# A two-block transformer on one core: x loaded in four pieces between the first weight halves, the positions loaded as rows and turned by small products, and the first quarters ordered by channel half

## The reference

```python
def rms_norm(x, g):
    y = xf * lax.rsqrt(jnp.mean(xf * xf, axis=-1, keepdims=True) + NORM_EPS)
    return (y * g.astype(jnp.float32)).astype(x.dtype)

def rope_tables(positions):
    inv_freq = ROPE_THETA ** (-jnp.arange(0, ROT_DIM, 2, dtype=jnp.float32) / ROT_DIM)
    ang = positions.astype(jnp.float32)[..., None] * inv_freq
    return jnp.cos(ang)[:, None], jnp.sin(ang)[:, None]

def moba_attention(xn, w_qkv, w_o, cos, sin):
    qkv = (xn @ w_qkv).reshape(b, s, 3, N_HEADS, HEAD_DIM)
    ...
xn = rms_norm(x, norm_mix[i])
y = moba_attention(xn, attn_w_qkv[i_attn], attn_w_o[i_attn], cos, sin)
```

## Time and profile before

| | before |
|---|---|
| median of 3 runs (lowest to highest) | 1083.42 us (1083.03 to 1083.55) |
| the profiled execution's own time | 1084.0 us |
| its span, first to last instruction | 1082.1 us |
| TensorE matmuls busy in the span | 1068.2 us (99%) |
| VectorE, ScalarE busy | 740.3 us (68%), 561.6 us (52%) |
| moved by DMA | 195.84 MB, mean 181 GB/s |

### The profile page before, as it was taken

The page is one execution under the profiler, slowest core; times in us unless marked ns, Lnnn a source line. Parts: engine busy times, 40 slices in busy tenths (PEclk is TensorE's granted clock), DMA queues, the critical chain, the costliest instruction groups (busy, mean ns, idle before and its releaser), DMA issues.

```text
span 1082.1 us, 15291 instructions
## 1 busy us (share of the span) xinstructions
PE 1068.2 (99%) x5810; PEld 908.3 (84%) x5810; DVE 740.3 (68%) x1044; ACT 561.6 (52%) x725; POOL 40.7 (4%) x61
## 2 busy tenths in 40 slices
PE   8999999999999999999999999999999999999997
PEld 6888888888888888889888888888889778888886
DVE  5756674655786656558897966666897879566665
ACT  5556443434455435346675554445654766444453
POOL 1000000000000000000000220000300200000000
PEclk9999999999999999999999999999999999999999
DMA  9953266465447465646533665657576324654651
GB/s 333 336 174 112 86 216 217 166 203 184 159 140 257 158 215 171 202 137 184 194 120 102 213 206 177 195 187 239 152 254 225 81 79 163 226 193 157 207 179 39
DMA packets 127163, 195.84 MB, mean 181 GB/s; under 512 B 6977, under 2 KB 97217, under 8 KB 126994
## 3 DMA queue, kind: packets, MB, share of 16 engines
q1 hardware_dynamic: 123904, 185.77, 51.6%
q0 software_dynamic: 3216, 9.51, 2.9%
q10 hardware_dynamic: 2, 0.00, 0.0%
HBM read 194.21 MB, written 1.05 MB: 180 GB/s over the span
## 4 chain that ended last, share of the span: by engine, by line
PE 94%; DVE 4%; ACT 1%; issue 1%; DVEq 0%; DMA 0%; ACTq 0%
PE ps L2108 26%; PE ps L2009 15%; PE ps L2011 15%; PE ps L2010 15%; PE ps L2111 13%; PE ps L2190 2%; PE ps L2229 1%; PE ps L2051 1%; PE ps L2192 1%; PE ps L2255 1%; PE ps L2641 1%; DVE act L1246 1%; PE ps L2288 1%; DVE wlo L1121 1%; PE ps L2469 0%
## 5 line engine op out<-in xcount | busy, mean ns | idle before, releaser
L2108 PE MATMUL ps<-act,whi 128*128 128x512 f32 x1200 | 424.7, 397 | 0.0
L1121 DVE TENSOR_TENSOR wlo<-raw,whi 128x2048 fp32r<-128x2048 f32 (+2 forms) x161 | 364.0, 2277 | 87.2 <-ACT whi L678 86.8
L2111 PE MATMUL ps<-act,wlo 128*128 128x256 f32 x1200 | 336.6, 281 | 0.0
L678 ACT ACTIVATE whi<-raw 128x2048 fp32r<-128x2048 f32 (+2 forms) x170 | 317.5, 1887 | 26.2 <-PE ps L2011 21.2
L2108 PEld LDWEIGHTS ps<-act,whi 128*128 128x128 f32 x1200 | 225.3, 188 | 54.0
L2111 PEld LDWEIGHTS ps<-act,wlo 128*128 128x128 f32 x1200 | 226.7, 189 | 2.0
L2011 PE MATMUL ps<-whi,hlo 128*128 128x512 f32 x400 | 157.3, 393 | 0.0
L2010 PE MATMUL ps<-wlo,hhi 128*128 128x512 f32 x400 | 156.7, 392 | 0.0
L2009 PE MATMUL ps<-whi,hhi 128*128 128x512 f32 x400 | 156.4, 391 | 0.1
L2009 PE MATMUL ps<-whi,act 128*128 128x512 f32 (+2 forms) x286 | 112.4, 393 | 1.5 <-DVE act L1821 0.6
L2011 PE MATMUL ps<-whi,act 128*128 128x512 f32 (+2 forms) x286 | 108.0, 378 | 0.0
(11 more groups left out here) (232 smaller groups left out, 1153.8 us busy)
## 6 DMA issues: line engine op xcount, KB each, us to landing
raw<-mlp_w_up_in SPq DMA_DIRECT2D x32, 1024.0 KB, 6.3
raw<-mlp_w_down_in SPq DMA_DIRECT2D x32, 1024.0 KB, 4.9
raw<-ffn_w_gate_in SPq DMA_DIRECT2D x22, 1024.0 KB, 5.3
raw<-ffn_w_up_in SPq DMA_DIRECT2D x22, 1024.0 KB, 5.4
raw<-ffn_w_down_in SPq DMA_DIRECT2D x22, 1024.0 KB, 4.8
raw<-attn_w_qkv_in SPq DMA_DIRECT2D x10, 1024.0 KB, 8.9
raw<-w_kv_shared_in SPq DMA_DIRECT2D x8, 1024.0 KB, 5.3
raw<-attn_w_o_in SPq DMA_DIRECT2D x4, 1024.0 KB, 4.9
```

The lines of the kernel that those rows point to most:

```text
L678: nc.scalar.activation(whi[:, s, 0:width], raw[:, s, 0:width], ACT.Copy).then_inc(hi_ready, 1)
L1121: nc.vector.tensor_tensor(wlo[:, s, 0:width], raw[:, s, 0:width], whi[:, s, 0:width].bitcast(F32), ALU.subtract).then_inc(lo_ready, 1)
L2108: nc.tensor.matmul(bank(b + f), lhsT=w[0][:, at:at + P], rhs=act[:, k, :, :].rearrange("p a t -> p (a t)"), start=k == 0, stop=False, skip ...
L2111: ins = nc.tensor.matmul(bank(b + f, 0, T), lhsT=w[1][:, at:at + P], rhs=act_hi[:, k, :], start=False, stop=k == KT - 1, skip_group_check= ...
```

## The change

SP loads x in four pieces of 256 KB, each one quarter, between the weight halves. The quarters of the first norm are now ordered by channel half: quarters 0 and 1 are the token tiles 0 and 1 of channels 0 to 511, quarters 2 and 3 those of the other channels. ACT's queue loads the two position arrays as rows of 256 integers on one partition, behind the gain row; POOL's two loads go. VectorE converts the 512 integers at the head of its list; TensorE turns them into columns by four products with a 1x1 one, and VectorE copies the four columns. The second half of the gain row is spread after the first quarter's transposes. Five identity products stand ahead of the first quarter, none later. `qkv_products` of chunk 0 takes one token tile after the other, with the transposes of quarters 1, 2 and 3 in between.

```diff
+        pos_row_i = arena[0:1, 0:512].bitcast(I32)
+        pos_row = arena[0:1, 512:1024]
...
-        BY_TILES = ("mix0", "mlp0", "mix1", "mlp1", "fpre0", "kvsrc", "fpre1")
+        BY_TILES = ("mlp0", "mix1", "mlp1", "fpre0", "kvsrc", "fpre1")
...
-            sp.dma_start(x[:, 0, :], x_rows[:, 0, :]).then_inc(x_loaded, 16)
+            def load_x(p):
+                h, t, cols = quarter("mix0", p)
+                sp.dma_start(x[:, t, cols], x_rows[:, t, cols]).then_inc(x_loaded[p], 16)
+
+            load_x(0)
             load_half(0, 0, first_half_loaded)
-            sp.dma_start(x[:, 1, :], x_rows[:, 1, :]).then_inc(x_rest_loaded, 16)
             load_half(0, 1, w_loaded[SLOT[0]])
+            load_x(1)
             load_half(1, 0, second_half_loaded)
+            load_x(2)
             load_half(1, 1, w_loaded[SLOT[1]])
+            load_x(3)
...
-            for n, name in enumerate(("positions", "positions_2")):
-                pool.dma_start(pos_i[:, n, :], a[name].rearrange("a (t p) -> p (a t)", p=P),
-                               allow_slow_non_contiguous=True).then_inc(pos_loaded, 16)
...
+            for n, name in enumerate(("positions", "positions_2")):
+                act.dma_start(pos_row_i[:, n * T:(n + 1) * T], a[name]).then_inc(pos_loaded, 16)
...
+            hi_part_of(0, 0, first_half_loaded, first_half_hi)
             copy_turned("mix0", (0,))
-            hi_part_of(0, 0, first_half_loaded, first_half_hi)
-            copy_turned("mix0", (1, 2))
             hi_part_of(0, 1, w_loaded[SLOT[0]], hi_ready)
             hi_part_of(1, 0, second_half_loaded, second_half_hi)
-            copy_turned("mix0", (3,))
+            copy_turned("mix0", (1,))
             hi_part_of(1, 1, w_loaded[SLOT[1]], hi_ready)
+            copy_turned("mix0", (2, 3))
...
+            dve.wait_ge(pos_loaded, 32)
+            nc.vector.tensor_copy(pos_row, pos_row_i).then_inc(pos_row_made, 1)
             dve.wait_ge(first_row_spread, 1)
...
+            nc.vector.tensor_copy(pos_f[:, :, :].rearrange("p n t -> p (n t)"), bank(7, 0, 2 * TT)).then_inc(pos_copied, 1)
...
-            dve.wait_ge(pos_loaded, 32)
-            link(nc.vector.tensor_copy(pos_f[:, :, :], pos_i[:, :, :]))
+            dve.wait_ge(pos_copied, 1)
...
+            spread_first_row(0)
+            pe.wait_ge(const_loaded, 16)
+            warm(5)
+            turn("mix0", parts=(0,))
+            spread_first_row(1)
+            pe.wait_ge(pos_row_made, 1)
+            for n in range(2 * TT):
+                ins = nc.tensor.matmul(bank(7, n, n + 1), lhsT=pos_row[:, n * P:(n + 1) * P], rhs=scale_row[0:1, 0:1],
+                                       start=True, stop=True)
...
-                    for h in range(2):
-                        pe.wait_ge(*((lo_ready, c + 1) if h else (half_lo, 1)))
-                        for t in range(TT):
-                            if h == 0:
-                                wait_acts("mix0", c + 1 + 2 * t)
+                    for t in range(TT):
+                        wait_acts("mix0", 2 * c + t + 1)
+                        for h in range(2):
+                            pe.wait_ge(*((lo_ready, c + 1) if h else (half_lo, 1)))
...
-                            if c == 0 and h == 0 and t == 1:
-                                turn("mix0", parts=(3,))
+                            if c == 0 and t <= h:
+                                turn("mix0", parts=(1 + h + t,))
```

More of the change, by code:

```diff
@@ L236, in two_blocks @@
         row_used = sem("row_used")
-        x_loaded = sem("x_loaded")
-        x_rest_loaded = sem("x_rest_loaded")
+        x_loaded = [sem(f"x_loaded{p}") for p in range(4)]
         second_half_loaded = sem("second_half_loaded")
@@ L246, in two_blocks @@
         pos_loaded = sem("pos_loaded")
+        pos_row_made = sem("pos_row_made")
+        pos_turned = sem("pos_turned")
+        pos_copied = sem("pos_copied")
         bias_loaded = [sem(f"bias_loaded{s}") for s in range(8)]
@@ L1616, in lo_part_of @@
                                         whi[:, SLOT[c], cols].bitcast(F32), ALU.subtract).then_inc(done, 1)
+            dve.wait_ge(pos_loaded, 32)
+            nc.vector.tensor_copy(pos_row, pos_row_i).then_inc(pos_row_made, 1)
             dve.wait_ge(first_row_spread, 1)
-            dve.wait_ge(x_loaded, 16)
-            dve.sem_inc(x_ready, 2)
+            dve.wait_ge(x_loaded[0], 16)
             first_gained(0)
+            lo_part_of(0, 0, first_half_hi, 1, first_half_lo)
+            split_turned("mix0", (0,))
+            dve.wait_ge(x_loaded[1], 16)
             first_gained(1)
-            split_turned("mix0", (0,))
-            dve.wait_ge(x_rest_loaded, 16)
+            lo_part_of(0, 1, hi_ready, 1, lo_ready)
+            dve.wait_ge(first_row_spread, 2)
+            dve.wait_ge(pos_turned, 1)
+            nc.vector.tensor_copy(pos_f[:, :, :].rearrange("p n t -> p (n t)"), bank(7, 0, 2 * TT)).then_inc(pos_copied, 1)
+            dve.wait_ge(x_loaded[2], 16)
             dve.sem_inc(x_ready, 2)
             first_gained(2)
-            lo_part_of(0, 0, first_half_hi, 1, first_half_lo)
             split_turned("mix0", (1,))
+            lo_part_of(1, 0, second_half_hi, 1, second_half_lo)
+            split_turned("mix0", (2,))
+            dve.wait_ge(x_loaded[3], 16)
+            dve.sem_inc(x_ready, 2)
             first_gained(3)
-            split_turned("mix0", (2,))
-            lo_part_of(0, 1, hi_ready, 1, lo_ready)
+            lo_part_of(1, 1, hi_ready, 2, lo_ready)
             dve.wait_ge(xs_ready, 4 * XSR["mix0"] + 4)
             release_row()
-            lo_part_of(1, 0, second_half_hi, 1, second_half_lo)
             split_turned("mix0", (3,))
-            lo_part_of(1, 1, hi_ready, 2, lo_ready)
             cursor[0] = 2
@@ L2031, in turn @@
             def turn(name, blocks=((0, 4), (4, 8)), parts=range(4)):
-                if name == "mix0" and 0 in parts:
-                    pe.wait_ge(ones_made, 1)
-                    pe.wait_ge(first_row_loaded, 16)
-                    for h in range(2):
[L2037 to L2040, removed]
                 for p in parts:
                     h, t, _ = quarter(name, p)
-                    if name == "mix0":
-                        for _ in range((3, 0, 3, 0)[p]):
-                            nc.tensor.matmul(bank(7, 0, P), lhsT=ident, rhs=ident, start=True, stop=True)
                     if name in BUSY:
@@ L2399, in ffn_layer, with spread_first_row, warm @@
                 last_downs(f, n0 + 31, n0 + 32, NF, then, (5, 6) if then else ())
-            turn("mix0", parts=(0, 1, 2))
+            def spread_first_row(h):
+                nc.tensor.matmul(bank(2 + h), lhsT=scale_row[0:1, 0:P], rhs=rows[0:1, 0, h * HALF:(h + 1) * HALF],
+                                 start=True, stop=True).then_inc(first_row_spread, 1)
+            def warm(n):
+                for _ in range(n):
+                    nc.tensor.matmul(bank(7, 0, P), lhsT=ident, rhs=ident, start=True, stop=True)
+            pe.wait_ge(ones_made, 1)
+            pe.wait_ge(first_row_loaded, 16)
+            spread_first_row(0)
[7 more added lines that the diff above has]
+                                       start=True, stop=True)
+            ins.then_inc(pos_turned, 1)
             def qkv_products(i, kh):
```

1 line of the change is left out of this document (removed).

## The result

The change makes the kernel slower: 1088.23 us (median of 6 runs, 1085.65 to 1088.56) against 1083.49 us of the kernel before (6 runs, 1083.03 to 1084.45). The forecast was 1083.7, with a range to 1085.9. The profiled execution took 1088.55 us with a span of 1086.1, against 1084.0 and 1082.1.

The account below looks back on a forecast made before the run. TensorE was taken to bound the kernel. Chunk 2's high part 0.79 later, less 0.17 for the conversion and 0.30 of cover, starts chunk 4 0.32 later: 1083.42 + 0.32 = 1083.7 us, range 1082.0 to 1085.9.

Parts of the forecast that it names:

- the other road: VectorE's path to the first product, through the first quarter's copy and low part: ready at 9.0, shorter than TensorE's.
- the rival of late positions: Positions land after 5.2 and hold VectorE's whole queue; at worst first product 2.5 later, 1086.2 us; chance 0.06.
- The new wait: TensorE idle ahead of chunk 4 until VectorE's copy of the first result: about 0.32 + 0.8 = 1.1 us.
- the second tile of x: Landed at 9.2; its late landing held the third quarter's gain product, hence the low part ahead of the first product.
- the 5.74 for 24 products: TensorE's time for 24 products and one more turn after the last quarter's turn at 16.71, ending about 22.8.
- TensorE goes faster at about 9.1: TensorE's step from lower to upper level comes at about 9.1, as in the earlier trace, after the second half-row's passes start.
- the position passes: Eight TensorE passes ahead of the first product, priced at the upper level: 0.90 us, first product at 10.14.
- from the first product to the last turn: TensorE's four groups of six products and turns in chunk 0: 6.57 us, last quarter turned at 16.71.
- the chain behind: From ScalarE's high part of chunk 2 to VectorE's copy ahead of chunk 4: 17.15 us without slack, less 0.17 for the conversion.
- the slow level: TensorE stays at its lower level through the one-row products: 1084.5 with no slow product, 1085.8 with six; chance 0.14.

Follow-up runs that it names:

- the control: The kernel before with chunk 4's high and low parts put ahead of the sine and cosine: 1083.79 us, ratio 1.0001.
- The pair of fillings: Changed kernel with both half-rows first, positions behind the last quarter, plus six products in TensorE's gap: identity 1086.08 us, one-row 1088.61 us.

## Why the prediction was wrong

**What held.** The first transposes start at 6.58, as forecast. The first quarter's low part ends at 8.31 + 0.69 = 9.00, as the other road had it. The conversion ended at 4.01, before the 5.2 at which it would cost (0.41 us, between its bounds), so the rival of late positions fell. From the last turn to chunk 2's high part it took 1.13 (forecast 1.12), and from there to chunk 4 17.19 (forecast 16.98). The new wait is 1.34 (forecast 1.1), released by VectorE's copy. Two readings that the time did not rest on were off: the second tile of x did not hold the first product (9.20 + 0.69 = 9.89 for the low part ahead of the gain product), and the 5.74 for 24 products, from which the 1.1 follows, stands in no row (24 x 0.227 = 5.45).

**The step that failed** is the sentence that TensorE goes faster at about 9.1, with the position passes priced at the upper level behind it. In the earlier trace rows the steps shrank at 9.10 behind identity products and transposes without a break; the prediction took over the time, while the change broke that work off at 7.57 with one-row products. The time was also that of one execution: the control's opening, the same, had its first short step at 12.10. The position products ran at the lower level: 1.63 us for the eight passes, the upper bound (to the digit by chance), not 0.90. They start 0.20 later than forecast, most of it the step behind the turns, so the first product is 0.93 late. The next terms were sized at the same pace: from the first product to the last turn 6.57 was forecast, and 9.08 measured. The first six products with their turn take 3.43 (11.07 to 14.50) instead of 1.85, the next six 2.46 instead of 1.50.

**The sum again.** Chunk 4 was forecast at 34.81. With 0.93 for the first product, 2.51 for products and turns, and 0.22 for the chain behind, it comes to 38.47, which is the row; and 38.47 - 34.49 = 3.98 is the 4.0 by which the span grew. For the span nothing else is needed. The times of the two profiled executions differ by 4.55; the other 0.55 lies outside the span (2.45 us against 1.9), and no row shows why.

**The rival that happened** was the slow level, given 0.14 and six slow products for 1085.8. Its mechanism was right and its size too small: ten products and one turn were slow in the profiled execution, where the range was ended at six products. By its own sum ten would be 0.32 + 0.73 + 10 x 0.227 = 3.3 us; the slow turn (0.36), the 0.20 and the 0.22 above were not in it. The pair of fillings, with the spread of the rises beside it, shows that one-row work in that place is what kept the level low. That the rise differs from execution to execution is seen in the profiles (9.10 and 12.10 for one opening); the wide ranges (1085.65 to 1088.56 with the change, 1083.72 to 1088.62 without position products) fit it, but how many products are slow in the runs without a profile was not seen. The Trainium skill, "TensorE: Matmul & The Clock Gate", in its section "The HAM clock gate", says that the number of slow products varies from run to run of one kernel; the two profiles of one opening agree. The same page's "Back-to-back issue gap" would have made the position products an estimated 0.2 us; the rows disagree, with 1.63 at the lower level and 0.97 at the upper.

## What to carry to other kernels

A change of TensorE's pace is tied to the work that leads up to it, not to its time in the old trace, and that time is one draw among several: when a change breaks off that work, price everything behind it at both levels, the slow one first. Work that is moved from in front of the first product to behind it gains only where an engine was idle; here TensorE had 1.1 us of idleness between its start and the first product (0.61 and 0.47), and a first product 2.3 us earlier was worth 0.2. Identity products that look like filling may hold the pace: leaving six out cost 0.8 us (1083.82 to 1084.66), just clear of noise.

## What the runs showed of the hardware

- Over one-row fp32 products no rise of the pace was seen: not in 2.31 to 4.28 or 7.57 to 11.07 of the change, nor in 2.9 us of one-row filling, with TensorE busy throughout. Once up, the pace was kept over 1.05 us of one-row work between products and over 0.75 us of idleness. It was lost within 0.8 us of products behind 1.1 us of one-row work and 1.25 us of idleness, and within 0.4 us of products behind 2.28 us of idleness. Behind 1.41 us of idleness the products were fast too, but whether the level had risen ahead of that idleness can't be told: the steps up to 9.08 us were long, and only the modelled end of the last turn speaks for it. Each of these is one profiled execution.
- A one-row fp32 pass of one column with its weight load took 0.204 us at the lower level and 0.12 at the upper, about as much as a pass of 128 columns and 128 rows (turns 0.204, identity products 0.113).
- With two loads of 4-byte pieces issued at 1.3 and 2.1 us the stream fell from 323 to 105 GB/s for two microseconds; issued later they left 333 there. It was not the pieces alone: issued at 11.3 and 12.1 us and in flight for 5.3 to 5.7 us, the same loads left 349 to 399 GB/s from 10.5 to 18.5. Behind a broadcast of a 2 KB row to all partitions the stream fell to 133 GB/s (7.5 to 8.5 us); in the version without that load it was 356 there.
